# Sampled forgetting attention: gates held as 12 head rows and added by matmuls, in place of 96 loaded rows and an addition on VectorE

## The reference

```python
F = jnp.cumsum(logf_all, axis=1)
F = F - F[:, -1:]
...
s = jnp.einsum('bqhd,bkhd->bhqk', qb, k).astype(jnp.float32) * (Dh ** -0.5)
s = s + jnp.transpose(Fqb, (0, 2, 1))[..., :, None] - FkT[:, :, None, :]
s = jnp.where((k_pos[None, :] <= qpb[:, None])[None, None], s, -jnp.inf)
p = jax.nn.softmax(s, axis=-1).astype(v.dtype)
return jnp.einsum('bhqk,bkhd->bqhd', p, v)
```

## Time and profile before

| | us |
|---|---|
| median of 3 runs | 3792.38 |
| range of the runs | 3789.47 to 3805.63 |
| the profiled execution | 3797.99 |
| its span, first to last instruction | 3796.3 |

### The profile page before, as it was taken

How to read it: one execution, slowest core, us unless ns; L and a number is a source line. 1 busy time by engine, 2 the same in 40 slices (tenths; PEclk the granted TensorE clock), 3 DMA queues, 4 the chain that set the end, 5 groups by cost and what they waited for, 6 DMA issues and landing times. The chain is left out here.

```text
span 3796.3 us, 49559 instructions
## 1 busy us (share of the span) xinstructions
PE 3209.6 (85%) x18461; PEld 2632.9 (69%) x18461; DVE 1380.2 (36%) x2385; ACT 984.6 (26%) x1866; POOL 297.1 (8%) x676
## 2 busy tenths in 40 slices
PE   6997655979999969979676888888487999996995
PEld 5886443779999958868574444444277999995884
DVE  3113533534444432241101444434144444443233
ACT  4221112422222223242201333333132222222222
POOL 0000000001000100000000011111300000010000
PEclk9996557989999989989887999999788999998997
DMA  5212323321111054451106999999442111114354
GB/s 190 91 71 79 106 52 130 112 89 68 68 68 68 35 171 148 129 215 76 60 28 207 333 350 351 350 340 370 146 166 92 65 68 68 68 46 159 116 177 166
DMA packets 280653, 540.02 MB, mean 142 GB/s; under 512 B 31602, under 2 KB 158899, under 8 KB 270499
## 3 DMA queue, kind: packets, MB, share of 16 engines
q1 hardware_dynamic: 251714, 453.45, 35.1%
q0 software_dynamic: 23584, 65.45, 4.5%
q10 hardware_dynamic: 5184, 18.88, 1.2%
HBM read 450.84 MB, written 86.85 MB: 142 GB/s over the span
## 5 line engine op out<-in xcount | busy, mean ns | idle before, releaser
L1534 PE MATMUL ps<-a_lo,ffn_up_w_hi 128*128 128x364 f32 (+1 forms) x2112 | 467.7, 330 | 28.5 <-DVE ffn_up_w_lo L1494 28.5
L1534 PE MATMUL ps<-a_hi,ffn_up_w_hi 128*128 128x364 f32 (+1 forms) x2112 | 467.0, 330 | 0.0
L1534 PE MATMUL ps<-a_hi,ffn_up_w_lo 128*128 128x364 f32 (+1 forms) x2112 | 466.7, 329 | 0.0
L1534 PEld LDWEIGHTS ps<-a_lo,ffn_up_w_hi 128*128 128x128 f32 x2112 | 367.6, 188 | 29.3 <-DVE ffn_up_w_lo L1494 29.3
L1699 PE MATMUL ps<-ffn_down_w_hi,ffn_down_y_lo 128*128 128x512 f32 x792 | 313.3, 396 | 73.3 <-DVE ffn_down_w_lo L1674 73.2
L1534 PEld LDWEIGHTS ps<-a_hi,ffn_up_w_hi 128*128 128x128 f32 x2112 | 367.6, 188 | 0.0
L1534 PEld LDWEIGHTS ps<-a_hi,ffn_up_w_lo 128*128 128x128 f32 x2112 | 367.4, 188 | 0.0
L1479 ACT ACTIVATE ffn_up_up<-ps 128x364 f32<-128x364 f32 (+1 forms) x264 | 101.2, 457 | 834.9 <-PE ps L1534 834.9
L1700 PE MATMUL ps<-ffn_down_w_hi,ffn_down_y_hi 128*128 128x512 f32 x792 | 311.7, 394 | 0.0
L1701 PE MATMUL ps<-ffn_down_w_lo,ffn_down_y_hi 128*128 128x512 f32 x792 | 311.3, 393 | 0.0
L1512 DVE TENSOR_SCALAR ffn_up_cp<-ffn_up_up,ffn_up_tp 128x1024 f32<-128x1024 f32 x88 | 71.7, 814 | 577.1 <-ACT ffn_up_us L1481 577.1
(11 more groups left out here) (312 smaller groups left out, 4564.7 us busy)
## 6 DMA issues: line engine op xcount, KB each, us to landing
attend_b_kr<-in_cache_kt SPq DMA_DIRECT2D x256, 384.0 KB, 6.8
attend_b_vr<-in_cache_v SPq DMA_DIRECT2D x256, 384.0 KB, 9.1
ffn_down_yr<-y_t SPq DMA_DIRECT2D x36, 1408.0 KB, 6.7
ffn_up_raw<-in_w_up SPq DMA_DIRECT2D x44, 1024.0 KB, 4.9
y_t<-ffn_up_y POOLq DMA_DIRECT2D x44, 544.0 KB, 3.0
ffn_down_raw<-in_w_down SPq DMA_DIRECT2D x44, 512.0 KB, 6.3
attend_b_fg<-fg SPq DMA_DIRECT2D x32, 384.0 KB
z_a<-project_z POOLq DMA_DIRECT2D x45, 256.0 KB, 2.3
```

What stands on the lines that cost most here:

```text
L1534: last = nc.tensor.matmul(g.ps[:, 3 * x + j, 0:cn], w, m[:, k, c0:c0 + cn], start=(k == 0 and n == 0), stop=(k == KD - 1 and n == 2))
```

## The change

The gates are loaded as what they are, 12 rows (one a head) of 1024 keys: 48 KB instead of 384 KB. Before its six matmuls, each `bs` unit now runs three matmuls that take these 12 rows as the moving operand and a 0/1 table `spread` (12 x 96: row h is 1 in the eight columns of head h) as weights, and so start the sums in the same PSUM rows; the six score matmuls add to them. VectorE's instruction stays, and adds a table `none` of zeros; it no longer waits for the gates' load, TensorE does. SyncE no longer waits for VectorE before the next load of gates. Two small VectorE instructions at the stage's start fill `none` and `spread`.

```diff
-    fg = g.sb("fg", [HT, FS, 2 * W])
+    fg, none = g.sb("fg", [H_FOX, FS, 2 * W]), g.sb("none", [HT, W])
+    spread = g.sb("spread", [H_FOX, H_FOX, DS])
...
             def load_f(b, x):
                 slot, _ = f_fill(b, x)
-                sp.dma_start(fg[:, slot], bc(fg_in_dram.rearrange("h b n -> b h n")[b][:, x * W:(x + 2) * W],
-                                             1, DS)).then_inc(f_in[slot], 16)
+                sp.dma_start(fg[:, slot], fg_in_dram[:, b, x * W:(x + 2) * W]).then_inc(f_in[slot], 16)
...
                     if x % 2 == 1 and i < DB * NG:
-                        wait_emptied(sp, u)
                         load_f(i // NG, i % NG)
...
+            pe.wait_ge(none_set, 2)
             pe.wait_ge(f_ready, 1)
...
                 slot, fill = k_fill(b, x)
+                f_slot, f_times = f_fill(b, x)
+                pe.wait_ge(f_in[f_slot], 16 * f_times)
+                for q in range(G):
+                    nc.tensor.matmul(g.ps[rows_of(q), bank, :], spread[:].rearrange("p h t -> p (h t)")[:, rows_of(q)],
+                                     fg[:, f_slot, (x % 2) * W:(x % 2) * W + W], start=True, stop=False)
                 pe.wait_ge(k_in[slot], 16 * GP * fill)
                 for c in pairs:
                     last = nc.tensor.matmul(g.ps[rows_of(c // 2), bank, :], qc[:, b, c],
-                                            kr[:, slot * GP:slot * GP + GP, c], start=(c % 2 == 0), stop=(c % 2 == 1))
+                                            kr[:, slot * GP:slot * GP + GP, c], start=False, stop=(c % 2 == 1))
...
             V = nc.vector
+            V.memset(none[:], 0.0).then_inc(none_set, 1)
+            V.tensor_copy(spread[:], bc(g.ident[0:H_FOX, 0:H_FOX], 2, DS)).then_inc(none_set, 1)
...
-                slot, fill = f_fill(b, x)
-                dve.wait_ge(f_in[slot], 16 * fill)
-                V.tensor_tensor_reduce(cols, g.ps[0:HT, bank_of(u), :], fg[:, slot, (x % 2) * W:(x % 2) * W + W], 1.0,
-                                       NEG, ALU.add, ALU.max, gm[:, x:x + 1]).then_inc(emptied(u), 1)
+                V.tensor_tensor_reduce(cols, g.ps[0:HT, bank_of(u), :], none[:], 1.0, NEG, ALU.add, ALU.max,
+                                       gm[:, x:x + 1]).then_inc(emptied(u), 1)
```

More of the change, by code:

```diff
@@ L2144, in attend_b @@
      fn_in, fn_done, qc_ready, scores_in, biased, masked, max_done, exp_done, o_in, ot_ready, o_turned, rsum_done,
-     o_done, group_max, bmax_done, bexp_done, sm_done, rs_done, v_used, vc_in, bo_in, bo_done) = (g.sem(n) for n in (
+     o_done, none_set, bmax_done, bexp_done, sm_done, rs_done, v_used, vc_in, bo_in, bo_done) = (g.sem(n) for n in (
          "ids_in ids_done tables_in knew_in krow_in mk_s_in mv_s_in zeroed f_turned f_ready k_turned kn_ready lfw_done "
          "fn_in fn_done qc_ready scores_in biased masked max_done exp_done o_in ot_ready o_turned rsum_done "
-         "o_done group_max bmax_done bexp_done sm_done rs_done v_used vc_in bo_in bo_done").split())
+         "o_done none_set bmax_done bexp_done sm_done rs_done v_used vc_in bo_in bo_done").split())
     o_stored = [g.pool_sem(f"o_stored{s}") for s in range(2)]
@@ L2578, in _ @@
             V = nc.vector
+            V.memset(none[:], 0.0).then_inc(none_set, 1)
+            V.tensor_copy(spread[:], bc(g.ident[0:H_FOX, 0:H_FOX], 2, DS)).then_inc(none_set, 1)
             dve.wait_ge(ids_in, 16)
             V.tensor_scalar(ids[:], ids[:], 0, cache_k.shape[0] - 1, ALU.max, ALU.min).then_inc(ids_done, 1)
+            dve.wait_ge(none_set, 2)
             dve.wait_ge(tables_in, 48)
```

## The result

| | before | after |
|---|---|---|
| median, us | 3790.93 (4 runs) | 3838.72 (4 runs) |
| range, us | 3786.93 to 3805.63 | 3834.28 to 3845.33 |
| profiled execution, us | 3797.99 | 3839.12 |
| its span, us | 3796.3 | 3837.4 |

The ratio of the runs is 1.012, with a 95% interval from 1.0089 to 1.0151; the medians lie 48 us apart: **48 us slower**. The forecast was +42 us, 3834 us.

What follows compares the result with a forecast made beforehand. TensorE's list was taken to bound the middle, with DMA close behind. Middle 55.9 - 8 - 4 = +44, opening +1, tail 0, small waits -3 gave +42 us on a 3792.4 us median: 3834 us, range 3806 to 3860.

Steps and rivals of the forecast that it cites:

- The bound: Middle, 545 us: TensorE's list sets the pace, matmuls busy 87%, DMA close behind; with matmuls side by side, chance 0.81.
- Rival A: Whole kernel: transfers are the bound, 31.5 us of DMA come off and the matmuls hide, 3761 us; chance 0.06.
- only 3.6 us could come back in the middle: Middle: of the 31.5 us of DMA saved, only TensorE's 3.6 us of waits for values can return.
- The rule that gives 12 DMA engines: Gates' load: 12 heads outermost spread it over 12 DMA engines, saving 42 us of those; not used in the sum.
- The three matmuls, 0.93 us each unit, 52.1 us in the middle: Middle, TensorE: two rounds, half the six score matmuls' 1.85 us; 56 units, plus 3.8 us at 1.2 GHz, 55.9 us.
- the change of shape: Each `bs` unit: fixed part of about 0.14 us for changing matmul shape, half inside 0.93, all in the high end.
- Rival B: `bs` units: the three matmuls run in a row, a unit grows by 3.15 us, about 3980 us; chance 0.05.
- Hidden behind waits, -8 us: Middle, before `bw`: waits for ScalarE's copy shrink by 4.6 us and those for values by 3.6 us.
- the -3 us for small waits: Elsewhere in TensorE's list: small waits that a later arrival covers, -3 us.
- The clock, -4 us: Middle: less TensorE idle time prevents some clock falls, -4 of 19 us, ends 0 and -17.
- The opening, +1 us: Opening: later `f` unit +4.3, seven units about +9, against 11.4 us of key waits; net +2, taken as +1.
- Rival C: Whole kernel: clock falls vanish, opening ends 5 us ahead, matmuls take 0.85 us; +19 us, 3811 us; chance 0.08.

Runs made afterwards that it cites:

- three further profiles with 12 rows: Profiles of kernels that feed the three matmuls or their single replacement 12 rows, beyond the changed kernel's first profile: middles of 600.5, 600 and 598.5 us.
- a second kernel with 128: Changed kernel with 128 rows fed and the first load of gates issued ahead of the twelve pages of keys: 3809.61 us, ratio 1.0046 against before.

## Why the prediction was right, point by point

- **The bound.** TensorE's list, and not the transfers, sets the pace of the middle. Right: with the load left at 96 rows the kernel is as slow as with 12 (3843 and 3839 us), and SyncE's waits for TensorE rose from 108 to 208 us in it, to 236 us in the changed kernel. Rival A is out, though the light load alone is worth 25 us. The prediction's sentence that only 3.6 us could come back in the middle was too strict: 9 us did, over half of them with the clock. The rule that gives 12 DMA engines stands in the Trainium skill, "DMA: Bandwidth & Descriptors", under "Why a DMA increments its semaphore by 16 and not by 1"; no row here shows single engines.
- **The three matmuls, 0.93 us each unit, 52.1 us in the middle.** Measured 0.984 us, 55.1 us. The missing 0.05 us fits the change of shape, of which I had half in the 0.93 and the whole in the high end; by 68 against 64 rows it is 0.10 us. Rival B (three in a row, 3.15 us) is out by the 0.98 us, and one matmul on 96 columns costs what three in strips do.
- **Hidden behind waits, -8 us.** TensorE's idle time in the middle fell by 13 us, at the two places that were named (8.9 to 3.5 us, 3.6 us to none) and in small parts elsewhere. Right, a little small; the -3 us for small waits belongs here.
- **The clock, -4 us.** Wrong in sign; this is the step that failed. I argued that less idle time means fewer falls. In the profile the clock of the middle fell from 0.96 to 0.92, from 44 to 97 us at 1.2 GHz by these rows. The 53 us more, with TensorE busy for nine tenths of them, cost an estimated 24 us. Busy rose by 76 us, of which the matmuls at full speed are 55 us and the clock the rest. In the three further profiles with 12 rows the clock is 0.94; that is 72 us at 1.2 GHz and by the same working a cost of 13 us. Over the whole program and all runs the time at 1.2 GHz went from 690 to 698 us to 713 to 716, some 20 us more, so the usual price is nearer 10 us than 24. The runs with more rows fed show that idle time isn't all that counts: the same matmuls with 128 rows left 638 to 659 us at 1.2 GHz, less than before the change, and with 12 rows the clock fell even where TensorE had hardly been idle.
- **The opening, +1 us.** The mechanism held: in the changed kernel the first `f` unit comes 23.9 us after the stage's start (2048.58 - 2024.64), before it was 20.0 us (2054.65 - 2034.66): +3.9 us, +4.3 had been forecast. The waits for keys vanished. The sum for the opening was -6 us in one profile and +2.5 us in the other, so the +1 us was neither borne out nor refuted.
- **The sum.** +42 us forecast, +48 us measured. The middle of the profile was 19 us longer than forecast (63 for 44), the opening was 6 us shorter, and 16 us came back in the stages around it, by chance. So part of the closeness of this one total is luck. With the +54 to +56 us of the other three profiles the middle is 10 to 12 us over the forecast, most of which is the clock's wrong sign. Rival C (most of it given back by the clock) is out for this kernel; with 128 rows fed something near it happened, 3805 us at a clock of 0.98 in the middle.

## What to carry to other kernels

- A full DMA queue doesn't mean that DMA is the bound: ask who waits for whom. Where loads are asked for in time and the queue that issues them waits for TensorE, bytes taken away are worth only the few waits that they end, and work put on TensorE in exchange is paid nearly in full.
- Price a small matmul by its passes and columns, not by the number of strips; the rows it feeds changed its hold by 0.10 us of 0.98. Three strips cost what one does; float32 takes two passes of records; a one-pass type cut the addition to 0.4 of it (0.98 to 0.38 us).
- When matmuls with a short contraction run often beside full ones, try feeding the same columns with 128 rows, zeros below. Here it took one fill with zeros at the stage's start and brought 34 us of 3839. The kernel stayed 11 us slower than before all the same.

## What was unexpected of the hardware

- Fed rows and clock: the same 192 small matmuls, fed 12, 68, 96 and 128 rows, left the program at 1.2 GHz for 716, 676, 666 and 638 us (659 in a second kernel with 128). The steps from 12 to 96 and to 128 are clear of the scatter, those between 64 and 128 are not. Why the rows bear on the clock is not shown by these runs, and neither is why 64 rows gave no gain in the medians while 68 did, beyond the 8 us of the shape.
- Shape: a matmul with 12 or 64 fed rows ahead of one with 128 costs 0.10 us more than one with 68, 96 or 128 rows there.
- Gains that don't add: the light load alone -25 us, the matmuls alone +49 us, both +48 us and +44 us in two measurements.
